# Mixture-of-experts rounds: steps of many-token and few-token experts interleaved, down products one step later, slot lists made ahead of the tokens' scaling

## What is computed

```
def moe_swiglu(h, w_router, w_gate, w_up, w_down):
    logits = h @ w_router                       # 256 x 8
    top_logits, top_idx = lax.top_k(logits, 2)  # two experts for each token
    gates = softmax(top_logits)
    ...
    for each expert e, for the rows xb routed to it:
        hb = silu(xb @ w_gate[e]) * (xb @ w_up[e])     # 1024 x 3584 each
        out[rows] += gates * (hb @ w_down[e])          # 3584 x 1024
```

## Time and profile before

| | us |
|---|---|
| median of three runs | 1929.48 |
| the profiled execution, device time | 1930.08 |
| its span in the trace | 1928.2 |
| TensorE busy | 1793.9 (93%) |
| VectorE busy | 1520.3 (79%) |
| ScalarE busy | 1233.1 (64%) |
| GpSimd busy | 257.7 (13%) |

### The profile page before, as it was taken

How to read it: one execution, slowest core, us unless ns; L and a number is a source line. 1 busy time by engine, 2 the same in 40 slices (tenths; PEclk the granted TensorE clock), 3 DMA queues, 4 the chain that set the end, 5 groups by cost and what they waited for, 6 DMA issues and landing times.

```text
span 1928.2 us, 23720 instructions
## 1 busy us (share of the span) xinstructions
PE 1793.9 (93%) x8738; PEld 1489.9 (77%) x8738; DVE 1520.3 (79%) x1806; ACT 1233.1 (64%) x1446; POOL 257.7 (13%) x297
## 2 busy tenths in 40 slices
PE   8989988899989899999899999999989998898887
PEld 7877877688879788888878877788777886777766
DVE  7775996858566655455778879988899889999998
ACT  6562145755664453434766778877788778888876
POOL 5113302314011000000008700010001000010100
PEclk9999999899999999999999999999999999999999
DMA  9422334324415255555159999999999999999996
GB/s 359 153 88 88 109 142 147 132 68 173 153 66 197 88 193 180 195 185 186 45 226 359 369 360 413 421 412 391 371 420 414 402 378 386 422 411 421 397 421 280
DMA packets 74298, 512.04 MB, mean 266 GB/s; under 512 B 9393, under 2 KB 9409, under 8 KB 14273
## 3 DMA queue, kind: packets, MB, share of 16 engines
q1 hardware_dynamic: 70736, 498.88, 66.0%
q0 software_dynamic: 3440, 11.58, 2.0%
HBM read 503.08 MB, written 7.36 MB: 265 GB/s over the span
## 4 chain that ended last, share of the span: by engine, by line
PE 57%; DVE 21%; DMA 10%; ACT 7%; issue 3%; POOL 1%; SPq 0%; DVEq 0%; ACTq 0%; POOLq 0%
PE psum L1112 31%; DVE low L1066 13%; DMA raw<-in_moe_weights 10%; PE psum L1506 6%; PE psum L1520 6%; PE psum L1513 6%; ACT high L1063 4%; DVE arena L2245 3%; PE psum L2086 2%; PE psum L1546 1%; PE psum L1551 1%; ACT h L1821 1%; PE psum L3902 0%; PE psum L3905 0%; PE psum L1717 0%
## 5 line engine op out<-in xcount | busy, mean ns | idle before, releaser
L1066 DVE TENSOR_TENSOR low<-raw,high 128x2048 fp32r<-128x2048 f32 x459 | 1038.9, 2286 | 232.2 <-ACT high L1063 228.3
L1063 ACT ACTIVATE high<-raw 128x2048 fp32r<-128x2048 f32 x459 | 873.5, 1911 | 319.0 <-PE psum L1112 156.0
L1112 PE MATMUL psum<-high,yT_high 128*128 128x512 f32 x776 | 223.8, 395 | 4.8 <-issue 1.9
L1112 PE MATMUL psum<-high,yT_low 128*128 128x512 f32 x776 | 219.3, 390 | 0.0
L1112 PE MATMUL psum<-low,yT_high 128*128 128x512 f32 x776 | 212.5, 390 | 0.5 <-DVE low L1066 0.5
L1112 PE MATMUL psum<-low,hT_high 128*128 128x512 f32 x656 | 184.4, 403 | 5.8 <-DVE low L1066 4.7
L1112 PE MATMUL psum<-high,hT_high 128*128 128x512 f32 x656 | 184.8, 404 | 5.3 <-issue 3.8
L1112 PEld LDWEIGHTS psum<-low,yT_high 128*128 128x128 f32 x776 | 145.5, 188 | 31.9 <-DVE low L1066 1.4
L1112 PEld LDWEIGHTS psum<-high,yT_low 128*128 128x128 f32 x776 | 145.6, 188 | 30.9
L1112 PEld LDWEIGHTS psum<-high,yT_high 128*128 128x128 f32 x776 | 142.0, 188 | 33.0 <-issue 4.4
L1112 PEld LDWEIGHTS psum<-low,hT_high 128*128 128x128 f32 x656 | 122.2, 191 | 47.7 <-DVE low L1066 23.0
(11 more groups left out here) (445 smaller groups left out, 2198.4 us busy)
## 6 DMA issues: line engine op xcount, KB each, us to landing
raw<-in_moe_weights SPq DMA_DIRECT2D x336, 1024.0 KB, 9.6
raw<-in_weights SPq DMA_DIRECT2D x132, 1024.0 KB, 4.9
raw<-in_weights SPq DMA_DIRECT2D x2, 896.0 KB, 4.5
raw<-in_weights SPq DMA_DIRECT2D x2, 768.0 KB, 6.1
x<-in_x SPq DMA_DIRECT2D x2, 512.0 KB, 4.2
raw<-in_weights SPq DMA_DIRECT2D x2, 512.0 KB, 3.7
base<-x POOLq DMA_DIRECT2D x1, 1024.0 KB, 6.6
rows<-arena POOLq DMA_DIRECT2D x1, 1024.0 KB, 5.0
```

The costliest lines, as they stand in the source:

```text
L1063: eng.activation(high, raw, ACT.Copy).then_inc(k.high_ready, 1)
L1066: eng.tensor_tensor(low, raw, high.bitcast(F32), ALU.subtract).then_inc(k.low_ready, 1)
L1112: last = pe.matmul(out, lhs[:, c, :], rhs[:, c, :], start=start and c == 0, stop=stop and c == chunks - 1)
```

## The change

The step order in a round becomes gate j, down j-2, turn j-1, up j, so down products stand two steps behind. `moe_order()` no longer puts whole rounds side by side: it takes the first 20 granules from round 0 alone, and after that picks item by item from the big and from the small experts (rounds 3 to 6) in proportion to what is left of each, so that both run out together; round 7 stands alone at the end. A rule keeps at least one product of the other kind between the last turn and the last down product of a round. The lists are split in three: `list_places` (28 instructions, no more behind the scaling, and waiting for the totals themselves instead of `totals_ready`), then the four indirect DMAs that write the places, then `list_order` (7 instructions), and only then the scaling and the store of the rows; `list_last` (the rest) stands behind the first fetch. `split_upto` is now also called ahead of the last turn.

```
 def round_order(t):
     last = FF_STEPS - 1
     order = []
-    for j in range(FF_STEPS + 1):
-        if j < FF_STEPS:
-            order += [(t, "gate", j)]
-        if 1 <= j <= last:
-            order += [(t, "turn", j - 1)]
-        if j < FF_STEPS:
-            order += [(t, "up", j)]
...
+    for j in range(FF_STEPS):
+        order += [(t, "gate", j)]
+        if j >= 2:
+            order += [(t, "down", j - 2)]
+        if j >= 1:
+            order += [(t, "turn", j - 1)]
+        order += [(t, "up", j)]
...
+    order += [(t, "down", last - 1), (t, "turn", last)]
+    if t != BIG - 1:
+        order += [(t + 1, "gather", 0), (t + 1, "gather", 1)]
+    return order + [(t, "down", last), (t, "out", 0)]

 def moe_order():
+    size = {"gate": 2, "up": 2, "down": 2, "down first": 1, "down second": 1}
     big = [item for t in range(BIG) for item in round_order(t)]
     small = [(BIG, "gather", 0), (BIG, "gather", 1)] + [item for t in range(BIG, N_EXPERTS) for item in round_order(t)]
-    for t in range(BIG):
-        order += round_order(t)
-        order += [(BIG, "gather", 0), (BIG, "gather", 1)] if t == 0 else []
-        order += round_order(BIG + t)
-    for t in range(2 * BIG, N_EXPERTS):
-        order += round_order(t)
+    beside_big = sum(size.get(kind, 0) for _, kind, _ in big) - ALONE
+    beside_small = sum(size.get(kind, 0) for t, kind, _ in small if t != LAST)
+    order, done_big, done_small = [], 0, 0
+    between = {False: True, True: True}
+    while big or small:
+        lead = done_big < ALONE or (done_big - ALONE) * beside_small <= done_small * beside_big
+        from_big = bool(big) and (lead or not small)
+        rows = big if from_big else small
+        other = small if from_big else big
+        if rows[0][1:] == ("down", FF_STEPS - 1) and not between[from_big] and other and done_big >= ALONE:
+            from_big, rows = not from_big, other
+        item = rows.pop(0)
...

 in moe_pool:
-    pool.wait_ge(k.gain_landed, 16)
-    for t in range(TILES):
-        pool.tensor_tensor(b.scaled[:, t, :], k.h[:, t, :], b.gain, ALU.mult).then_inc(k.rows_scaled, 1)
-    pool.wait_ge(k.rows_scaled, TILES)
-    pool.dma_start(rows.rearrange("(t p) d -> p t d", p=P), b.scaled).then_inc(k.rows_stored, 16)
...
-    moe_lists(k, pool, b)
...
+    list_places(k, pool, b)
     pool.wait_ge(k.places_cleared, 16)
     for t in range(TILES):
         for choice in range(2):
...
+    list_order(k, pool, b)
+    pool.wait_ge(k.gain_landed, 16)
+    for t in range(TILES):
+        pool.tensor_tensor(b.scaled[:, t, :], k.h[:, t, :], b.gain, ALU.mult).then_inc(k.rows_scaled, 1)
+    pool.wait_ge(k.rows_scaled, TILES)
+    pool.dma_start(rows.rearrange("(t p) d -> p t d", p=P), b.scaled).then_inc(k.rows_stored, 16)
     pool.wait_ge(k.places_written, 16 * 2 * TILES)
...
     fetch(BIG)
+    list_last(k, pool, b)

 def list_places(k, pool, b):
+    k.wait_released(pool, "places")
+    k.wait_released(pool, "totals")
...

 in moe_scalar and moe_vector:
-        if (kind, j) != ("turn", FF_STEPS - 1):
-            done = split_upto(k, act, done, MOE_GRANULES, index)
+        done = split_upto(k, act, done, MOE_GRANULES, index)
```

More of the change, by code:

```diff
@@ L383 @@
 LAST = N_EXPERTS - 1
+ALONE = 20
 def round_order(t):
@@ L405, in round_order @@
-    if t not in (LAST, "more"):
-        order += [(t, "out", 0)]
-    return order
+    if t in (LAST, "more"):
+        return order + [(t, "down first", last - 1), (t, "turn", last), (t, "down second", last - 1), (t, "down", last)]
+    order += [(t, "down", last - 1), (t, "turn", last)]
+    if t != BIG - 1:
+        order += [(t + 1, "gather", 0), (t + 1, "gather", 1)]
+    return order + [(t, "down", last), (t, "out", 0)]
 def moe_order():
+    size = {"gate": 2, "up": 2, "down": 2, "down first": 1, "down second": 1}
@@ new lines, in moe_order @@
+    beside_small = sum(size.get(kind, 0) for t, kind, _ in small if t != LAST)
[9 more added lines that the diff above has]
+        item = rows.pop(0)
+        n = size.get(item[1], 0)
+        if from_big:
+            done_big += n
+        else:
+            done_small += n
+        if item[1:] == ("turn", FF_STEPS - 1):
+            between[from_big] = False
+        if n > 0:
+            between[not from_big] = True
+        order.append(item)
@@ L3670, in moe_pool, with sum_last, list_places @@
     pool.dma_start(k.x[:, :, :], base[0:SEQ, :].rearrange("(t p) d -> p t d", p=P)).then_inc(k.x_back, 16)
-def moe_lists(k, pool, b):
-    steps = k.engine_steps["pool"]
[L3676 to L3685, removed]
+def sum_last(steps, pool, a, out):
+    n = N_EXPERTS // 2
+    while n > 1:
+        steps.link(pool.tensor_tensor(a[:, :, 0:n], a[:, :, 0:n], a[:, :, n:2 * n], ALU.add))
+        n //= 2
+    steps.link(pool.tensor_tensor(out, a[:, :, 0], a[:, :, 1], ALU.add))
+def list_places(k, pool, b):
+    steps = k.engine_steps["pool"]
+    k.wait_released(pool, "places")
+    k.wait_released(pool, "totals")
     steps.link(pool.tensor_scalar(b.key, k.totals, float(N_EXPERTS), None, ALU.mult))
@@ L3689, in moe_lists, with list_order @@
     steps.link(pool.tensor_scalar(b.above, b.above, 0.0, None, ALU.is_gt))
-    sum_last(b.above, k.expert_round)
+    sum_last(steps, pool, b.above, k.expert_round)
+    hot = k.one_hot.rearrange("p t k e -> p (t k) e")
+    steps.link(pool.tensor_tensor(b.by_token, hot, over_groups(k.expert_round, 2 * TILES), ALU.mult))
+    sum_last(steps, pool, b.by_token, k.round_of)
+    for t in range(TILES):
+        steps.link(pool.tensor_tensor(b.by_token[:, 2 * t:2 * t + 2, :], k.one_hot[:, t, :, :], over_groups(k.place[:, 0, t, :], 2), ALU.mult))
+    sum_last(steps, pool, b.by_token, k.place_of)
+    steps.link(pool.tensor_scalar(k.beyond, k.round_of, float(BIG), float(HALF), ALU.is_lt, ALU.mult))
+    steps.link(pool.tensor_scalar(k.beyond, k.beyond, float(HALF), None, ALU.add))
+    steps.link(pool.tensor_tensor(k.beyond, k.place_of, k.beyond, ALU.subtract))
+    steps.link(pool.tensor_scalar(k.beyond, k.beyond, 0.0, None, ALU.is_gt))
+    steps.link(pool.tensor_scalar(k.slot_of, k.round_of, float(P), None, ALU.mult))
+    steps.link(pool.tensor_tensor(k.slot_of, k.slot_of, k.place_of, ALU.add))
+    steps.link(pool.tensor_tensor(k.to_spare, k.spare_place, k.slot_of, ALU.subtract))
+    steps.link(pool.tensor_tensor(k.to_spare, k.to_spare, k.beyond, ALU.mult))
+    steps.link(pool.tensor_tensor(k.slot_of, k.slot_of, k.to_spare, ALU.add))
+    steps.link(pool.tensor_scalar(k.place_row[:, :], k.slot_of, -1.0, None, ALU.add))
+    steps.link(pool.tensor_copy(k.entry, k.own_entry.rearrange("p (t k c) -> p t k c", t=TILES, k=2)))
+    pool.wait_ge(k.share_done, 1)
+    steps.link(pool.tensor_copy(k.entry[:, :, :, 2], k.share.rearrange("p (t k) -> p t k", t=TILES)))
+def list_order(k, pool, b):
+    steps = k.engine_steps["pool"]
+    experts = k.count[:, 0:N_EXPERTS]
     steps.link(pool.tensor_tensor(b.above, over_groups(k.expert_round, N_EXPERTS), over_columns(experts, N_EXPERTS), ALU.subtract))
@@ L3693, in moe_lists, with list_last @@
     steps.link(pool.tensor_tensor(b.above, b.above, over_groups(experts, N_EXPERTS), ALU.mult))
-    sum_last(b.above, b.key)
+    sum_last(steps, pool, b.above, b.key)
     pool.tensor_copy(k.order[:, :], b.key).then_inc(k.order_ready, 1)
+def list_last(k, pool, b):
+    steps = k.engine_steps["pool"]
     steps.link(pool.tensor_scalar(k.cap, k.expert_round, float(BIG), float(HALF), ALU.is_lt, ALU.mult))
@@ L3700, in moe_lists @@
     steps.link(pool.tensor_tensor(k.place[:, 1, :, :], k.place[:, 0, :, :], over_groups(k.cap, TILES), ALU.subtract))
[L3702 to L3714, removed]
     steps.link(pool.tensor_scalar(k.in_last, k.round_of, float(N_EXPERTS - 1), None, ALU.is_equal))
@@ L3733, in moe_lists @@
     pool.sem_inc(k.lists_ready, 1)
+    for i in range(2):
+        k.wait_filled(pool, ("moe", "first", i))
+    for tile in range(TILES):
+        for half in range(2):
+            pool.tensor_scalar(b.placed[:, tile, HALF * half:HALF * (half + 1)], k.count[:, 0:HALF], 1.0, k.last_place[:, tile:tile + 1],
+                               ALU.add, ALU.is_equal).then_inc(k.last_placed, 1)
 def moe_wait_scatter(k, sp, i):
@@ L4145, in moe_vector @@
     for index, (t, kind, j) in enumerate(MOE_ORDER):
-        if (kind, j) != ("turn", FF_STEPS - 1):
-            done = split_upto(k, v, done, MOE_GRANULES, index)
+        done = split_upto(k, v, done, MOE_GRANULES, index)
         step(Spot(t), kind, j)
```

13 lines of the change are left out of this document (1 added, 12 removed).

## The result

The changed kernel takes 1913.55 us (median of four runs, 1912.5 to 1915.86), the one before 1929.1 beside it: a ratio of 0.9923, 95% interval 0.9906 to 0.994, 15 us less. Timed again later beside three of the experiments it gave 0.9944 (0.9928 to 0.9961), 11 us less. The forecast was 1916. The profiled execution has a span of 1911.1 us, 17.1 under that of before.

The account below looks back on a forecast made before the run. Big rounds were taken as TensorE-bound, small ones as DMA-bound, and the merged stretch as DMA-bound. 1930.1 - 21.1 (interleaving) + 6.8 (DMA lost to the lists) = 1915.8, said as 1916 us; own range 1907 to 1925, wider range 1898 to 1931.

Parts of the forecast that it names:

- DMA as the bound: Merged stretch, granule 22 of round 0 to round 7: DMA-bound at 413 GB/s, 707.5 us instead of 728.6, gain 21.1 us.
- The round ends: At round ends, TensorE's idle time is covered by the other stream and lies inside DMA's time: worth nothing.
- The splits ahead of the last turn: Calling the splits ahead of a round's last turn changes no instruction: between 0 and 1 us.
- The lag: Down products one step later: TensorE's wait for hidden values goes, but inside DMA's time, so worth nothing by itself.
- The lists: Start of round 3, near 1083: its rows land at 1087.2 to 1089.4, and 6.8 us of DMA are lost.
- The sum: Whole kernel: 1930.1 - 21.1 + 6.8 = 1915.8 us, with 707.5 and 6.8 for the merged stretch.
- The order of the experts: SyncE's wait ahead of load 22: `order` comes at 1058.5, load due at 1065.5; costs nothing, 7 us to spare.
- The Trainium skill's rule on the shared port: Scaling beside VectorE's lows: by the rule 4.4 us of waiting instead of 2.2, the time 2 us longer.
- The rival of slower lists: Start of round 3: rows land at 1112.6, TensorE and DMA stand 23 us more, 1939; decides from 1104; chance 0.08.
- No averaging: Merged stretch: three split buffers cannot carry slack; granules stay 2.80 and 2.56 us, 721 us, total 1929; chance 0.16.
- DMA at 421: Merged stretch: DMA keeps 421 GB/s despite row traffic, rows come by 1083, total 1899; chance 0.12.
- the clock: Merged stretch: short waits lower TensorE's clock; TensorE bounds from a mean of 0.89 down, 1949 at 0.87; chance 0.05.

Follow-up runs that it names:

- relieving TensorE: The changed kernel without the pass of the tokens' low parts in the big rounds (8 matmuls a granule instead of 12): 1915.66 us, ratio 0.9953.
- relieving DMA: The changed kernel loading only three quarters of each expert granule (1536 of 2048 columns): 1888.08 us, ratio 0.9805.
- late gathers: The changed kernel with the next expert's gathers also held back until a product of the other kind stands behind the last turn: 1906.93 us, ratio 0.9909.
- the lag alone: The kernel before with down products one step later, new round ends and splits ahead of the last turn; whole rounds, old lists: 1959.24 us, ratio 1.0177.
- alone with the old ends: The kernel before with down products one step later, last turn between the halves of down 5, no splits ahead of it: 1926.31 us, ratio 1.0008.
- without it: The changed kernel with down products one step behind, as in the kernel before, inside rounds 0 to 6: 1911.19 us, ratio 0.9938.
- the second timing's profile: Profile of the unaltered changed kernel when timed again beside three of the other kernels: 1913.37 us, ratio 0.9944.
- the order alone: The changed `MOE_ORDER` with the lists of the kernel before, behind the scaling in one block: 1931.56 us, ratio 1.0032.
- the full change: The changed kernel with all parts of the change, against the kernel before: 1913.55 us, ratio 0.9923; timed again 1913.37 us, ratio 0.9944.
- the relieved kernel: The kernel before without the pass of the tokens' low parts in the big rounds: 1916.63 us, ratio 0.9943.

## Why the prediction was right, point by point

**DMA as the bound, 413 GB/s, 707.5 us.** Right. The rate of the whole stretch is 413 and the chain is the one described; relieving TensorE gave nothing and relieving DMA gave 21 us in the stretch. But it is not 410 to 416 throughout, as the signs had it: the windows are at 417 to 423, or well below. And what the 413 is made of I had partly wrong; I put it on the row traffic. Against 421 the stretch loses 13 to 14 us (710.4 - 293.4/0.421 = 13.5). The windows with row traffic alone lose 4.6, and 1.5 are lost at the start. The window at 1435 loses 4.4, of which 1.2 to 1.7 may be its own row traffic (with late gathers the same 25 us lose 1.7), and the 6 us from 1786 to 1792, where DMA falls to 199 GB/s, lose 3.2. So some 6 us are the two round ends and some 6 the traffic.

**The round ends, at nothing.** Half right. That they must be covered is shown by the 33 us of the lag alone. But the cover has two holes of 3.6 us, which I didn't see in the order. At one a product wants the bank of the other stream's last turn before VectorE has read it; at the other, where rounds 2 and 6 end together, the rule fails and round 6's last down stands right behind its own turn and the gathers. "It is inside DMA's time" failed as well: ScalarE stands 5 to 6 us with TensorE, the raw buffers fill, and DMA loses time.

**The splits ahead of the last turn, at 0 to 1 us.** Not shown, and doubtful. No kernel changes them alone, and in both traces above a granule's low stands between the last turn and its hidden values, 2.3 us of a pause of 3.6.

**The lag, at nothing.** Right in both settings (1.0008 alone with the old ends; 0.9938 without it against 0.9944 with it).

**The lists, rows at 1087 to 1089, 6.8 us of DMA lost.** The mechanism was right, its price too high. The fetch was issued at 1076.75 where the sum had 1077.0, or 1079.2 with the mutual waiting; that it met so closely is luck. The parts differ (the places' list is 5 us faster in the less busy start, the read back waits 10.2 us instead of 5.9) and cancel, and in the second timing's profile the same kernel issues it at 1070.95. The landing took 8.7 and not 10.1. DMA lost about 1.5 us (396 GB/s from 1085 to 1110), not 6.8, since TensorE stood for 4.2 us in two pieces and not 8.4; the sign of one idle gap of 6 to 10 us was not met.

**The sum, 714.3 for the stretch against 710.4.** The sum lost 20.3 us against 421 GB/s (13.5 in the 413 and 6.8 at the start), the kernel 13.5 in all. The start was priced 5.3 too high; the rest of the 413 lost 12.0 instead of 13.5; and the measured bytes, with the rounding of the rates, make 2.9 us more: 714.3 - 5.3 - 1.5 + 2.9 = 710.4. That the 413 came out to the unit is luck in part, for it was chosen as a rate of row traffic and holds the round ends and the start as well. The upper bound of the forecast's own range, 408 GB/s and the full gap, adds up to 1926.7 and not 1925.

**The order of the experts, 7 us to spare.** Right: `order` at 1053.6, and SyncE's queue shows no wait for it.

**The Trainium skill's rule on the shared port (SBUF — State Buffer, Who interferes with whom).** The added time was 2.2 by the row and 4.4 by the rule; the fetch came at neither, 0.3 us before the sum without any. The scaling took 8.87 us, against 8.79, in an unbroken row of lows, and it was VectorE that paid: the two lows beside it took 4.06 and 3.90 us instead of 2.3.

**The rival of slower lists.** It was to decide from rows that land 14 to 15 us late. In the order alone they came 14.6 us later than in the full change (1100.05 against 1085.47), and the kernel was 0.3% slower than before: the distance was about right, though in absolute time it lies before the 1104 that the rival named. Its price (23 us) was not, since waiting DMA engines bring the list and the rows faster.

**No averaging.** Refuted, most clearly by TensorE relieved: if a big granule in the mixture still took its 2.80 us, the relief would have brought some 30 us (104 granules, 0.3 each), and it brought none. A granule takes 2.61 us in the full change (710.4/272), not the 2.65 of 2.80 and 2.56 mixed (721/272), and 2.51 with the loads cut. The floor of 2.43 under DMA was too low, however; it took each engine's work by itself.

**DMA at 421, and the clock.** Neither came. Five of the windows with row traffic stay at 401 to 412 GB/s. The mean granted clock is 0.99 in the stretch, far from the 0.89 that would have made TensorE the bound; where it did fall behind a pause, in the second timing's profile, the stretch was 3.1 us longer.

## What to carry to other kernels

Before interleaving a phase bound by one engine with a phase bound by another, multiply the bytes of both out at the rate of the transfer-bound one: here the compute-bound rounds already loaded at 94% of it, which capped a gain that looked like 54 us at 21. An interleaved order wants its second stream early, so the work that the second stream waits for (lists, fetches) has to be moved with it, or the change is a loss. And where two streams share a ring of banks, count who takes the bank of the longest chain next: a rule that puts a product between two items of one stream does not protect the ring. Print the order and read its ends, too: the rule here failed at the one place where both streams end.

## What the runs showed of the hardware that I had not expected

GpSimd's small instructions were slower where VectorE was busier. With the same instructions ahead of it, the first fetch came at 1102.54 us in the kernel before and at 1125.72 with TensorE relieved, where VectorE had been busy for 67.8 of the 70 us from 1030 to 1100 instead of 62.6; relieving one engine delayed another by 23 us, of which 1.2 were there when the lists began. Windows of the relieved kernel and of the kernel before:

```profile
1030.00:1100.00 70.00, 61.08 (x245) 44.51 (x243) 67.84 (x38) 58.22 (x40) 66.17 (x49) 0.95 1.01 403
```
```profile
1030.00:1100.00 70.00, 70.00 (x319) 57.95 (x317) 62.59 (x35) 52.26 (x34) 56.10 (x52) 1.00 0.97 368
```

GpSimd is busy for 10 us more in the same 70 with three instructions fewer. The Trainium skill, SBUF — State Buffer, Who interferes with whom, has an exclusive lock between VectorE with two SBUF inputs and GpSimd's reads, which fits; that it is this lock and not another was not tried, and DMA and ScalarE were busier in that stretch as well. Second, small indirect fetches landed in 4.3 us when the weights' loads stood and in 8.7 to 10.6, by the medians of the other traces, beside them, so a late list costs less than its distance in a busy trace.
